# Two small moves in three engines' queues of an attention stage, and round start addresses for the buffers

## What is computed

```python
def odd_mixer(x, mix_norm, w_qkv, q_norm, k_norm, w_out):
    proj = rms_norm_2(x, mix_norm) @ w_qkv
    q, k, v = jnp.split(proj, [1024, 1280], axis=-1)
    q = apply_rope(rms_norm_2(q.reshape(B, S, 16, 64), q_norm), cos, sin)
    k = apply_rope(rms_norm_2(k.reshape(B, S, 4, 64), k_norm), cos, sin)
    # 4 query heads share a head of k and of v
    s = jnp.einsum('bqgrd,bkgd->bgrqk', q, k) * 64 ** -0.5
    p = jax.nn.softmax(s, axis=-1)
    return jnp.einsum('bgrqk,bkgd->bqgrd', p, v).reshape(B, S, 1024) @ w_out
```

## Time and profile before

| | before |
|---|---|
| median of 3 runs | 1661.09 us (1661.05 to 1663.91) |
| the profiled execution | 1662.19 us |
| its span, first to last instruction | 1660.9 us |
| mean granted TensorE clock | 0.994 |
| DVE busy | 974.3 us (59%) |
| ACT busy | 787.9 us (47%) |
| POOL busy | 70.5 us (4%) |
| DMA | 289.33 MB, mean 174 GB/s |

### The profile page before, as it was taken

One profiled execution on the slowest core, in us unless ns is written; L12 is line 12 of the kernel. 1 busy time (PEld: TensorE's weight loads), 2 busy tenths in 40 slices (PEclk: granted clock), 3 DMA queues, 4 the chain that ended last, 5 costly groups with the idle time before them and its releaser, 6 DMA issues.

```text
span 1660.9 us, 18705 instructions
## 1 busy us (share of the span) xinstructions
PE 1636.8 (99%) x7962; PEld 1337.1 (81%) x7962; DVE 974.3 (59%) x1008; ACT 787.9 (47%) x961; POOL 70.5 (4%) x100
## 2 busy tenths in 40 slices
PE   9999999999999999999999999999999999899999
PEld 7877877888888888798888879977788887578887
DVE  5646675654455545646745475878555457755453
ACT  5445444543444434546534355745443445744342
POOL 0000000100001000100100010010000002000000
PEclk9999998999999999999999999999999999999999
DMA  9444542454545545453645454433454544145451
GB/s 361 182 183 175 184 155 102 184 196 177 203 177 204 193 174 193 175 196 127 228 180 194 173 184 182 171 111 87 181 212 177 197 166 163 64 152 192 173 193 48
DMA packets 51967, 289.33 MB, mean 174 GB/s; under 512 B 14215, under 2 KB 14855, under 8 KB 19114
## 3 DMA queue, kind: packets, MB, share of 16 engines
q1 hardware_dynamic: 51596, 287.54, 47.4%
q10 hardware_dynamic: 288, 0.59, 0.1%
HBM read 287.06 MB, written 1.05 MB: 173 GB/s over the span
## 4 chain that ended last, share of the span: by engine, by line
PE 91%; DVE 4%; ACT 3%; issue 1%; POOL 1%; DMA 0%; SPq 0%; DVEq 0%; ACTq 0%
PE ps L536 87%; PE ps L640 2%; PE ps L545 1%; ACT wh L1286 1%; DVE wl L1969 1%; DMA raw<-in_w 0%; ACT scg L1866 0%; DVE tmp L2000 0%; DVE x L2002 0%; PE ps L1144 0%; POOL st L2727 0%; POOL st L2724 0%; DVE scg L2652 0%; ACT tmp L1305 0%; DVE smg L2639 0%
## 5 line engine op out<-in xcount | busy, mean ns | idle before, releaser
L1969 DVE TENSOR_TENSOR wl<-raw,wh 128x2048 fp32r<-128x2048 f32 x256 | 579.8, 2287 | 156.1 <-ACT wh L1286 156.0
L536 PE MATMUL ps<-wh,xTh 128*128 128x512 f32 x1408 | 559.1, 397 | 3.4 <-DVE xTl L2008 1.3
L536 PE MATMUL ps<-wh,xTl 128*128 128x512 f32 x1408 | 551.3, 392 | 0.0
L536 PE MATMUL ps<-wl,xTh 128*128 128x512 f32 x1408 | 550.5, 391 | 0.0
L1286 ACT ACTIVATE wh<-raw 128x2048 fp32r<-128x2048 f32 x256 | 481.2, 1908 | 7.6 <-PE ps L536 4.4
L536 PEld LDWEIGHTS ps<-wh,xTh 128*128 128x128 f32 x1408 | 265.8, 189 | 69.1 <-issue 7.2
L536 PEld LDWEIGHTS ps<-wh,xTl 128*128 128x128 f32 x1408 | 265.6, 189 | 56.7
L536 PEld LDWEIGHTS ps<-wl,xTh 128*128 128x128 f32 x1408 | 266.0, 189 | 53.2
L2724 POOL TENSOR_SCALAR st<-st 128x1 f32<-128x1 f32 (+2 forms) x46 | 30.3, 659 | 1403.4 <-ACT tmp L1305 817.0
L1349 ACT ACTIVATE sgf<-ps,st 128x256 f32<-128x256 f32 x22 | 10.5, 476 | 104.1 <-PE ps L536 104.0
L1349 ACT ACTIVATE sge<-ps,st 128x256 f32<-128x256 f32 x22 | 10.4, 475 | 97.6 <-PE ps L536 97.6
(11 more groups left out here) (340 smaller groups left out, 2276.8 us busy)
## 6 DMA issues: line engine op xcount, KB each, us to landing
raw<-in_w SPq DMA_DIRECT2D x256, 1024.0 KB, 4.8
gains<-in_rows SPq DMA_DIRECT2D x18, 512.0 KB, 4.1
raw<-in_w SPq DMA_DIRECT2D x8, 512.0 KB, 10.0
nab<-in_rpb SPq DMA_DIRECT2D x32, 32.0 KB, 2.5
out_x<-x SPq DMA_DIRECT2D x2, 512.0 KB, 2.6
x<-in_x ACTq DMA_DIRECT2D x1, 512.0 KB, 6.0
x<-in_x SPq DMA_DIRECT2D x1, 512.0 KB, 9.9
nabfirst<-in_rpb SPq DMA_DIRECT2D x16, 32.0 KB, 2.7
```

The costliest lines, as they stand in the source:

```text
L536: return pe.matmul(o, lhs, rhs, start=start, stop=stop, skip_group_check=False)
L1969: TT(wl[:, p % RAW, :], raw[:, p % RAW, :], wh[:, p % RING, :].bitcast(F32), ALU.subtract).then_inc(*lo(p))
```

## The change

Four calls move, each within its engine's list in the odd mixer, and two unused buffers are laid between the others.

```diff
@@ build @@
+        sb("gap0", [128, 224])
         with ExitStack() as same:
             raw = sb("raw", [128, RAW, 2048], F32, same)
...
         ones2 = sb("ones2", [2, 128], F32R)
 
+        sb("gap1", [128, 72])
         stats = {}
@@ tensor_program, odd @@
                 out(0, 0)
                 turn(2, 1)
+                out(0, 1)
                 for i in range(3, 7):
                     scores(i + 1)
-                    out(i - 3, 1)
+                    if i > 3:
+                        out(i - 3, 1)
                     values(i - 1)
@@ scalar_program, odd @@
                 scores(0)
                 q_stat(1, 0)
+                ring.fill(1, p0 + 3)
                 scores(1)
...
                 turn(1, 1)
-                scores(3)
                 q_turn(1, 1)
                 values(1)
                 turn(2, 0)
-                ring.fill(1, p0 + 3)
+                scores(3)
                 for i in range(3, 7):
@@ vector_program, odd @@
                 scores(2)
                 q_rope(1, 1)
+                scale(2)
                 values(0)
                 q_sum(1, 1)
-                scale(2)
                 scores(3)
```

## The result

| | before | after |
|---|---|---|
| median | 1662.0 us (4 runs, 1661.05 to 1663.91) | 1649.36 us (4 runs, 1648.51 to 1650.21) |
| profiled execution, its span | 1662.19, 1660.9 | 1648.8, 1647.5 |
| mean granted clock | 0.994 | 0.997 |

The runs of both are from one chip. The ratio is 0.9927 (95% interval 0.9915 to 0.9939): 12.6 us less. The forecast was 1648.6, and the time lies in its range.

The account below looks back on a forecast made before the run. PE bounds the kernel, busy 1636.8 of 1660.9 us. Reorder 6.8 plus padding 5.7 make 12.5 us, taking the median from 1661.09 to 1648.6 us, range 1644.5 to 1656.5.

Parts of the forecast that it names:

- The order: Odd mixer: moving steps on ACT, DVE and PE removes waits and half-clock stretches, 6.8 us, bounds 4.9 to 7.2.
- ACT's split in its idle gap: Odd mixer, ACT: the 1.94 us split of piece 224 fits where ACT stands still 2.46 us, so costs nothing.
- DVE's 4.62 us: Odd mixer, DVE: its 4.62 us wait for ACT's split of piece 224 would be gone.
- PE's 0.43 and 2.32: Odd mixer, PE: the waits of 0.43 us before turn(2,0) and 2.32 us before turn(2,1) would be gone.
- what is late next: Odd mixer: DVE's chain becomes the late one, and PE waits 1.14 us for turn(3,1) instead of 1.91.
- rival 2: Odd mixer: reorder gives half, half clock costing 1.6 us a drop; 1651.8 or 1657.5; two drops or no padding: 0.08.
- The placed schedule: Odd mixer: steps placed engine by engine reach turn(4,1) at 1435.1 where it was 1442.28, 7.2 us earlier.
- the cover by out(0, 1): Odd mixer, PE: out(0,1) covers pair 3's exponentials, so scores(4) starts at 1423.8 instead of 1425.31.
- The padding: FFN matmuls: hT as weights goes from 233 to xTh's 227 ns by its address, 5.7 us, bounds 0 and 8.5.
- on a multiple of 64 bytes: FFN and oT buffers: hT and oT, 32 bytes past such an address, move onto one; hT then reaches xTh's pace.
- the 0.02 a run behind transposes: FFNs: the padding's gain in each of 78 runs behind transposes, bounded by nothing and 0.056 us; 1.6 us together.
- rival 3: Slower: the common address makes the xTh stream take hT's pace, costing 26.6 us, to 1680.9; chance 0.06.

Follow-up runs that it names:

- e1: The changed kernel without its two unused buffers, so the new order alone; 1654.35 us, ratio 0.9957 to the kernel before.
- e5: The changed kernel with PE's out(0, 1) back behind scores(4); 1648.62 us in one execution.
- e2: The kernel before with both unused buffers added and the old order kept; 1657.02 us, ratio 0.9967 to the kernel before.
- e3: The kernel before with only the second unused buffer, gap1, added; 1655.88 us, ratio 0.9965 to the kernel before.
- e4: The changed kernel with the buffers of FFNs b to f shifted by 32, 64, 128, 256 and 1024 bytes; 1652.77 us in one execution.
- e12: The changed kernel with wh moved 128 bytes, the others except FFN a's kept at a multiple of 256 from wl; 1656.39 us in one execution.
- e8: The changed kernel with pair 3's exponentials on ACT back ahead of qTg, values(1) and turn(2,0)'s copy; 1651.52 us in one execution.
- e6: The changed kernel with ACT's split of piece 224 put back behind turn(2,0)'s copy; 1651.83 us in one execution.

## Why the prediction was right, and where it was not

**The order: right.** Forecast 6.8 us, found 7.14 by position and 7.6 by the medians of e1. Each step came as placed: ACT's split in its idle gap, DVE's 4.62 us gone, PE's 0.43 and 2.32 gone, "what is late next" at turn(3,1) with 1.19 us against 1.14. The clock was kept, as for the 1.24 us of the earlier trace rows; rival 2 did not happen. That the argument from the earlier trace rows was safe is not shown: the 0.71 us wait of before at 1128.26 (last section) went with a fall to 0.50. The placed schedule (7.2) was nearer than the sum of the terms (6.4) or my 6.8 between them. The total of 12.5 against 12.6 is closer than its parts: by PE's positions they are 7.1 and 5.5, forecast 6.8 and 5.7.

**One step in it failed: the cover by out(0, 1).** The text lets out(0, 1) "cover the exponentials of pair 3", as a part of the gain. e5 shows that with out(0, 1) back behind scores(4) PE meets the same 1.1 us one step earlier. DVE's chain from the split to the peaks of pair 4 sets the time of turn(3,1)'s copy, and PE's order in front of it only chooses where to wait. In after ACT's exponentials of pair 4 wait only 0.23 us for these peaks, straight behind ACT's next split, so ACT's own queue is nearly as late; a faster DVE alone would gain no more than that 0.23.

**The padding: right size, wrong rule.** Forecast 5.7 us; e2 measured 4.9 (the interval of its ratio is 3.7 to 7.3 us), and 5.5 by PE's positions. The mechanism of the forecast, hT reaching xTh's pace of 227 ns by its address, is what happened. The step that failed is "on a multiple of 64 bytes". e3 and e4 put in its place: as long as wh and wl share their offset, hT's distance from them must be a multiple of 256, and no absolute address matters. That the padding worked in b to f all the same is luck: it put hT on a multiple of 2048, as it did wh, which meets both rules. With the right rule FFN a nearly drops out of the sum. From start to start the hT matmuls of b to f take 312.3 us before and 307.5 in e2, 4.8 less: the 45 runs of twelve behind a gate (the trace has nine in each FFN, the prediction counted eight) x 0.071 = 3.2, those behind transposes 1.4, the split ones 0.1. FFN a gives 0.2 and the even mixer's oT 0.1. The forecast had 3.6, 1.6 and 0.5. So the 0.02 a run behind transposes was well guessed (measured 0.024), and the split runs were mis-sized: in b to d one half of six gains 0.04 us (1.40 to 1.36) and the other loses as much (1.50 to 1.54). In the earlier trace rows and the addresses in the text both rules were to be had: xTh and wh were both 1152 past a multiple of 2048, hT 32 past a multiple of 64. I noticed the shared offset, as an argument against rival 3, and did not try it as the rule.

The rule that I weighed against it speaks of two independent read ports (the Trainium skill, "TensorE: Matmul & The Clock Gate", section "Step-by-step: what each phase is for"). By it the padding is worth nothing. e2 and e4 show otherwise: 2.725 against 2.80 us for the same twelve matmuls, by the operands' distance alone. That the two reads meet at a port is not shown by any run.

**Rival 3: price wrong, idea not empty.** xTh and wh kept their common offset and their 227 ns, as said against it. But e12 shows that xTh's stream does slow down at an unequal distance, by 7.7 us in all and not by the 26.6 of the rival. The collision goes the other way round from how the rival put it: unequal distances cost, equal ones do not.

## What to carry to other kernels

Where PE is the bound and loads and streams back to back, compare the start-to-start time by operand; if one operand is slower, look at its distance from the streamed ones modulo 256 bytes before looking at its absolute address. In a list of steps written by hand, find the engine whose chain sets the next wait before moving another engine's steps around it: three moves on ACT and DVE carried all of the gain, the one on PE none. Here a schedule placed step by step on all engines was a better forecast (7.2 us) than the waits summed up (6.4). Where two executions of kernels differ by about 1 us, compare the stretches at half clock first: in these profiles they alone moved the span by 0.7 and 1.2 us.

## What was not expected of the hardware

- A matmul's pace depends on where two operands lie relative to each other: 227 ns at equal offsets modulo 256 bytes, and 233 to 235 in the mean of twelve at offsets of 32, 64, 96 (FFN a of before), 128 and 224 bytes (b to f of before), which does not grow with the offset; only e12, where wh and wl differ too, shows a mean in between (229, b to f).
- A wait's length alone does not tell whether the clock falls. Behind the 1.91 us of e2 the granted clock was 0.50, the 1.2 GHz level, from 1431 to 1433; in e8 it stayed at 1.00 behind 1.89, in e6 behind 1.54 and 1.66. In e2, as in the earlier trace rows, the 1.91 us came 10 us behind a wait of 2.33 and a stretch at 0.50. Nor does the code around the wait fix it: behind the same wait ahead of the same matmul, at 1128.26 in before (0.71 us) and 1125.04 in after (0.70), the clock fell to 0.50 in the profiled execution of before and in e8's, and stayed at 1.00 in the twelve others. What decides was not tried.
